# Hybrid attention and expert block on one core: the first tile's v row moved from the end of each place to its start, on TensorE

## The reference, cut to what matters

```python
def expert_block(s0):                                  # 128 tokens
    hs, es, gs = hf[s0:s0+128], ef[s0:s0+128], gf[s0:s0+128]
    act = gelu(einsum('cd,ced->ce', hs, u[es]))        # a dot product for each pick
    return einsum('ce,ced->cd', gs * act, v[es])       # a weighted sum of v rows
```

## Time and profile before

| | |
|---|---|
| median of 3 runs | 2338.18 us (2337.74 to 2341.37) |
| the profiled execution | 2335.3 us, its span 2333.6 us |
| PE busy | 1991.9 us, 85% of the span |
| DVE, ACT, POOL busy | 1159.1, 360.5, 746.2 us |
| moved by DMA | 828.56 MB, mean 355 GB/s |
| v rows on PE in the places (line 1458) | 1024 records, 471.6 us |
| v rows on PE in the loop (line 1504) | 1024 records, 498.6 us |
| weight tiles of both tiles (line 1412) | 768 records, 371.4 us |

### The profile page before, as it was taken

How to read it: one execution, slowest core, us unless ns; L and a number is a source line. 1 busy time by engine, 2 the same in 40 slices (tenths; PEclk the granted TensorE clock), 3 DMA queues, 4 the chain that set the end, 5 groups by cost and what they waited for, 6 DMA issues and landing times.

```text
span 2333.6 us, 15961 instructions
## 1 busy us (share of the span) xinstructions
PE 1991.9 (85%) x5203; PEld 921.4 (39%) x5203; DVE 1159.1 (50%) x2049; ACT 360.5 (15%) x951; POOL 746.2 (32%) x660
## 2 busy tenths in 40 slices
PE   1789999899989989999888799889787777778777
PEld 0335464444434434455333334334333333333233
DVE  6756224561431327777624525623656555555642
ACT  0001011111221114334200102111111011101100
POOL 2103000010000024556422324423844645464550
PEclk9889889999999988999989999989988898989888
DMA  9978636885879788999999999999999999999995
GB/s 349 367 268 299 241 104 237 314 331 178 289 270 365 245 325 306 421 420 421 417 391 391 408 378 403 418 400 381 422 422 422 421 422 421 422 422 422 421 422 225
DMA packets 188040, 828.56 MB, mean 355 GB/s; under 512 B 16612, under 2 KB 22936, under 8 KB 112196
## 3 DMA queue, kind: packets, MB, share of 16 engines
q0 software_dynamic: 91648, 637.57, 67.2%
q1 hardware_dynamic: 94228, 186.28, 22.6%
q10 hardware_dynamic: 2096, 3.85, 0.4%
HBM read 825.52 MB, written 2.13 MB: 355 GB/s over the span
## 4 chain that ended last, share of the span: by engine, by line
PE 56%; DMA 35%; DVE 5%; issue 2%; POOL 2%; ACT 1%; SPq 0%; DVEq 0%; POOLq 0%; ACTq 0%
DMA arena<-in_peer_v_dram,idx_now 17%; PE PS L1458 12%; PE PS L1040 12%; PE PS L1412 12%; PE PS L1504 12%; DMA arena<-in_ada_w_dram 7%; DMA arena<-in_peer_w_q_dram 4%; DMA arena<-in_w_branch_nsa_dram 4%; DMA arena<-in_w_out_dram 3%; POOL arena L580 2%; DVE arena L1614 2%; DVE arena L1560 2%; PE PS L1209 1%; PE PS L1238 1%; DMA arena<-in_cmp_w_dram 1%
## 5 line engine op out<-in xcount | busy, mean ns | idle before, releaser
L1504 PE MATMUL PS<-arena 128*128 128x512 f32 x1024 | 498.6, 651 | 138.5 <-DMA arena<-in_peer_v_dram,idx_now 138.5
L580 POOL DMA_INDIRECT arena<-in_peer_v_dram,idx_now x256 | 352.4, 1376 | 618.4 <-PE PS L1458 371.0
L1458 PE MATMUL PS<-arena 128*128 128x512 f32 x1024 | 471.6, 606 | 15.9 <-DMA arena<-in_peer_v_dram,idx_now 15.9
L1412 PE MATMUL PS<-arena 128*128 128x512 f32 x768 | 371.4, 629 | 68.9 <-DMA arena<-in_peer_w_q_dram 22.8
L2039 DVE CUSTOM_DVE_ANT_0 arena<-arena 128x2048 f32<-128x2048 f32 x128 | 291.8, 2292 | 243.7 <-DMA arena<-in_peer_u_dram,idx_now 243.5
L1040 PE MATMUL PS<-arena 128*128 128x512 f32 (+1 forms) x912 | 399.1, 591 | 0.2 <-ACT arena L681 0.2
L1504 PEld LDWEIGHTS PS<-arena 128*128 128x128 f32 x1024 | 212.5, 210 | 424.6 <-issue 412.4
L580 POOL DMA_INDIRECT arena<-in_peer_u_dram,idx_now x256 | 313.5, 1225 | 166.4 <-issue 71.3
L2013 DVE CUSTOM_DVE_ANT_0 arena<-arena 128x2048 f32<-128x2048 f32 x128 | 290.9, 2288 | 49.5 <-DMA arena<-in_peer_u_dram,idx_now 46.4
L1458 PEld LDWEIGHTS PS<-arena 128*128 128x128 f32 x1024 | 195.5, 196 | 256.4 <-issue 233.1
L1412 PEld LDWEIGHTS PS<-arena 128*128 128x128 f32 x768 | 148.0, 199 | 259.3 <-issue 184.5
(11 more groups left out here) (247 smaller groups left out, 1159.7 us busy)
## 6 DMA issues: line engine op xcount, KB each, us to landing
arena<-in_ada_w_dram POOLq DMA_DIRECT2D x96, 1024.0 KB, 7.7
arena<-in_w_in_dram SPq DMA_DIRECT2D x112, 512.0 KB, 5.2
arena<-in_w_out_dram SPq DMA_DIRECT2D x64, 512.0 KB, 7.5
arena<-in_peer_w_q_dram SPq DMA_DIRECT2D x64, 512.0 KB, 9.3
arena<-in_w_branch_nsa_dram SPq DMA_DIRECT2D x32, 512.0 KB, 10.6
arena<-in_w_branch_mla_dram SPq DMA_DIRECT2D x32, 512.0 KB, 8.9
arena<-mod_rows SPq DMA_DIRECT2D x7, 1024.0 KB, 19.0
arena<-in_x_dram SPq DMA_DIRECT2D x4, 1024.0 KB, 8.5
```

Of the source, the lines that this page charges most:

```text
L580: pool.indirect_dma_start(dst, None, tab, bass.IndirectOffsetOnAxis(ap=idx_now[:, now, e:e + 1], axis=0)).then_inc(landed, 16)
L1412: ins = nc.tensor.matmul(PS[:, 4 + j % 3, :], lhs[:, 2 * w + k, :], tile[:, k, :], start=first and k == 0, stop=last and k == 1)
L1458: ins = nc.tensor.matmul(PS[:, k, :], diag[i % 8], Vrow0[i % RING0][:, k * NC:(k + 1) * NC], start=(i == 0), stop=False, skip_group_check= ...
L1504: ins = nc.tensor.matmul(PS[:, 4 + k, :], diag[e % 8], Vrow[e % RING][:, k * NC:(k + 1) * NC], start=(first and e == 0), stop=False, skip_ ...
```

## The change

At each place PE takes its v row first, then the second tile's piece, where it took the piece first and the v row last. Nothing else is changed, and the instructions of DVE, ACT, POOL and SP keep their order.

```diff
             for s in range(SLOTS):
+                if s >= LAG:
+                    v_row0(s - LAG)
                 if s < MIX1:
                     second_attention(s)
...
                 if s == SC_SLOT:
                     score_experts(1, 3)
-                if s >= LAG:
-                    v_row0(s - LAG)
```

## The result

The changed kernel took 2388.74 us (median of 4 runs, 2382.85 to 2398.89), the kernel before 2337.96 us beside it (4 runs, 2334.05 to 2341.37). The ratio is 1.0217, interval 1.0193 to 1.0242: 50.8 us slower. The profiled execution took 2391.16 us.

What follows compares the result with a forecast made beforehand. PE and DMA were taken as level in places 8 to 31, the DMA as bound later. Waits 33 plus clock 24, less 11.4 from the store, plus 2.0, gave 47 us: 2385 us, range 2350 to 2404.

Steps and rivals of the forecast that it cites:

- the clock: Attention stretch: PE runs slower after 3.2 us waits, 2.4 us for each of ten batches, 24 us up to v row 44.
- the store's gift: At v row 44: bytes under way fall from 6.2 to about 1.4 MB, giving back 11.4 us of DMA work.
- the order in the projection stretch: From place 56 on: earlier v rows may fill DMA holes, at most 26 us; nothing taken, 10 us kept for the range.
- The cover and its chain: Attention stretch: each batch's first v row waits for diagonals, mostly 3.2 us; 34.7 us, net 33, up to v row 44.
- what I said of batch 1: First batch, place 4: it waited for its first dots before too, so nothing was taken for it.
- The rival with waits and a full clock: Attention stretch: waits open but the clock stays at 2.4 GHz; 21.6 us slower, 2360 us; chance 0.20.
- v row 51: End of places 48 to 55: 57 us late at v row 44, then 2.0 us more with batch 13.
- the chain of place 87: Projection stretch: the same chains in places 87 and 119 cost some 2 us each on PE with 14% idle: nothing.
- the rival that expected a gain of 13 us there: Projection stretch: earlier v rows keep gathers going during weight waits, half of 26 us back; 2325 us; chance 0.05.
- The rule on a table's drain: ACT's table switches: a 1.38 us drain would lengthen twelve waits by some 15 us, about 2400 us; rejected from the trace.

Runs made afterwards that it cites:

- The kernel with the cover kept in the attention stretch: Against the kernel before: v row first in the attention stretch except each fourth place, last from place 56 on; 2337.28 us, ratio 0.9992.
- the kernel with the products: Changed kernel plus some 3.0 us of zero-adding products ahead of the v row in each fourth place, 8 to 52; 2375.53 us, ratio 1.0145 to before.
- attn_only: Against the kernel before: v row first in places 4 to 55 only, last from place 56 on; 2384.01 us, ratio 1.0194.
- not_84_to_92: Against the changed kernel: v row behind the piece again in places 84 to 92; 2381.40 us, ratio 1.0163 to the kernel before.

## Why the prediction came out as it did

The forecast of 2385 us met 2388.74, and the mechanism was as told; but two of its terms (the clock, the store's gift) were too large and one (the order in the projection stretch) was missing, and they nearly cancel.

- **The cover and its chain: right.** Twelve waits, by ACT line 957, between 921 and 1179 us. A wait of 3.2 us was forecast for batches 2 to 9: the trace has 2.92 us of idle time, and 3.09 by the starts. Batch 10: 1.8 forecast, 1.44 measured; batches 11 and 12: 3.65 and 3.34. The eleven up to v row 44 are 31.4 us idle, about 33 by the starts, where 34.7 was forecast. The kernel with the cover kept in the attention stretch has the loss back to 0. Wrong was what I said of batch 1: PE did not wait there before, and waits 2.92 us now; it cost next to nothing by v row 4, so that taking nothing for it came out by luck.
- **The clock: right in kind, too large.** 2.4 us for each of ten batches up to v row 44 were taken, 24 us, and 2.4 more for batch 13. Between v row 4 and v row 44 the first v rows of batches 2 to 11 took 1.40, 1.43, 1.44, 1.45, 1.70 and 2.87 us above 3.67 in six and nothing more in four (one of them batch 10, where no fall was forecast): 10.3 us. Batches 12 and 13 add 1.7 each, behind v row 44. A fall was priced too high, 2.4 us against 1.7 in the mean of eight, and the count was the step that failed: rows 7 showed two waits of over 3 us and a fall after both, and I took that for all. By v row 51 the falls come to 13.7 us of 26.4 forecast; the kernel with the products gives 12.1, or some 13.5 without what its block in place 40 adds. The rival with waits and a full clock was refuted by the granted clock of 0.92 to 0.96, and by the 13 to 17 us that the products brought back.
- **The store's gift: right, a little large.** 11.4 us forecast from 6.2 down to 1.4 MB under way; the masses came out as forecast. The gift is 7.9 us where the order is changed in the attention stretch alone and 10.6 where plain work makes the delay.
- **v row 51: forecast too late.** 57 us at v row 44 and 2.0 more were forecast, 59 us; it was 42.5 and 47.4.
- **The projection stretch: the missing term.** Nothing was taken for the order, and the stretch was to be 545 less 11 us. It came out 1.0 us longer than before, so the gift of 8 us is lost again. One place is shown to cost a part of it: the chain of place 87, which I had put at 2 us on a PE with slack, held PE for 5.65 us in place 88 and opened a hole in the DMA; what I had left out are the 4 us of DVE's own work ahead of the coefficients. (The other, of place 119, took 1.50 us.) The u rows' buffers, which I had only on the side of gains (rows fetched earlier), cost POOL 71.0 us of waits for DVE in the stretch, 4.6 before. The kernel with the change in that stretch alone is 3.5 us over (0 to 7), not faster: the rival that expected a gain of 13 us there is out. What makes up the rest of the lost gift stays open.
- **The sum.** Forecast 59 − 11.4 = 47.6; measured 47.4 + 1.0. The forecast was 11.6 us too high in the first part and 12.4 us too low in the second; that they cancel is luck.
- **The rule on a table's drain.** The Trainium skill (ScalarE: Activation LUTs, section What ACT_TABLE_LOAD costs) puts about 1.38 us of drain on a switch of tables. The changed kernel's rows agree with those of before, against the rule: the copy ends at 943.30, the load starts at 943.32, and the gelu 0.02 us behind the load's end. By the rule the waits would have been about 4.3 us, an estimate (2.92 + 1.38), and they were 2.92.

## What to carry to other kernels

Before an engine's steps are reordered, look at what stands between the step that starts a chain through other engines and the step that needs its end: that work is the chain's cover, and one v row of 3.6 us in each fourth place was worth the whole 45 us of the attention stretch here. Where an order must expose such a wait, shorten the chain on the other engine, or give PE zero-adding work in the gap; the latter brought back the part that the clock takes, 12 us by v row 51. And where gathers go through one in-order queue, an earlier release of one kind of buffer is only worth what the other kind allows: POOL just moved its wait from PE's buffers to DVE's.

## What the runs showed that was not expected

- Twelve waits of the same origin, eleven of 2.9 to 3.3 us, behind the same work: the clock fell behind eight of them. In places 8 to 32 it fell behind every second one (periods of 24.6 and 23.2 us in turn), and then in 36, 44, 48 and 52. The traces of attn_only and not_84_to_92, with the same waits, have the falls at the same eight v rows, so it is no accident of one execution. What decides it was not tried.
- A mixed order (v row first in three of four places) costs 26 to 29 us in the projection stretch where first in all places costs 3.5 by the runs of that kernel (9 in the changed one's profile, against the gift alone) and last in all nothing. A change that is harmless at both ends can be the worst in the middle.
- The point where the places start, far ahead of the edit, moved over 15 us between single profiled executions of kernels that are alike up to there. Spans of two profiled executions are thus no measure for a change of this size; distances from a common point inside them are.
